# Gated recurrence, first head group: one filling piece behind each pair of heads instead of two behind all four

## What is computed

```python
def step(state, inp):                      # one chunk of 64 tokens
    qc, kc, vc, gc = inp
    b = jnp.cumsum(gc, axis=2)
    diff = b[:, :, :, None, :] - b[:, :, None, :, :]
    decay = jnp.exp(jnp.minimum(diff, 0.0)) * tri[:, :, None]
    A = jnp.einsum('bhtsd,bhsd->bhts', qc[:, :, :, None, :] * decay, kc)
    o = (jnp.einsum('bhts,bhsv->bhtv', A, vc)
         + jnp.einsum('bhtd,bhdv->bhtv', qc * jnp.exp(b), state))
...
o = o * lax.rsqrt(jnp.mean(o * o, axis=-1, keepdims=True) + RMS_EPS)
```

## Time and profile before

| what | value |
|---|---|
| median of 3 runs | 2115.13 us (2115.03 to 2115.35) |
| profiled execution, its own time | 2115.07 us |
| its span in the profile | 2113.3 us |
| granted TensorE clock, mean | 0.999 of full speed |
| PE (matmul) busy | 2089.2 us, 99% of the span |
| DVE busy | 894.8 us, 42% |
| ACT busy | 789.8 us, 37% |
| POOL busy | 868.0 us, 41% |

### The profile page before, as it was taken

How to read it: one execution, slowest core, us unless ns; L and a number is a source line. 1 busy time by engine, 2 the same in 40 slices (tenths; PEclk the granted TensorE clock), 3 DMA queues, 4 the chain that set the end, 5 groups by cost and what they waited for, 6 DMA issues and landing times.

```text
span 2113.3 us, 33496 instructions
## 1 busy us (share of the span) xinstructions
PE 2089.2 (99%) x13820; PEld 1741.6 (82%) x13820; DVE 894.8 (42%) x1653; ACT 789.8 (37%) x1611; POOL 868.0 (41%) x680
## 2 busy tenths in 40 slices
PE   8999999999999999999999999999999999999998
PEld 7878888778978888778888888888888888888886
DVE  6173565535373465526432211433422612222264
ACT  5424335554423325455422222345433432222244
POOL 4633433232543433233354444343444345454423
PEclk9999999999999999999999999999999999999999
DMA  7522223122222223122242332242233133332222
GB/s 247 178 65 80 78 67 100 41 80 80 80 82 80 77 68 100 41 81 70 76 144 83 118 98 83 89 135 80 66 114 100 61 110 101 109 108 92 100 70 90
DMA packets 98679, 196.65 MB, mean 93 GB/s; under 512 B 3680, under 2 KB 12256, under 8 KB 98144
## 3 DMA queue, kind: packets, MB, share of 16 engines
q1 hardware_dynamic: 95072, 183.25, 26.6%
q10 hardware_dynamic: 3456, 11.27, 1.5%
HBM read 192.41 MB, written 2.10 MB: 92 GB/s over the span
## 4 chain that ended last, share of the span: by engine, by line
PE 59%; ACT 1%; DVE 0%; issue 0%; DVEq 0%
PE ps L902 18%; PE ps L903 18%; PE ps L904 18%; PE ps L1017 1%; PE ps L1157 1%; PE ps L1025 0%; PE ps L1034 0%; PE ps L1180 0%; PE ps L1200 0%; PE ps L1189 0%; PE ps L1070 0%; PE ps L1052 0%; ACT L1581 0%; PE ps L974 0%; PE ps L1210 0%; PE ps L1062 0%
## 5 line engine op out<-in xcount | busy, mean ns | idle before, releaser
L851 POOL TENSOR_TENSOR wl<-raw,wh 128x512 fp32r<-128x512 f32 (+2 forms) x676 | 867.8, 1307 | 1220.6 <-ACT wh L1255 1210.8
L1255 ACT CAST wh<-raw 128x512 fp32r<-128x512 f32 (+2 forms) x692 | 380.7, 604 | 773.3 <-PE ps L904 672.8
L902 PE MATMUL ps<-xh,wh 128*128 128x512 f32 (+1 forms) x1376 | 514.2, 374 | 1.2 <-issue 1.2
L904 PE MATMUL ps<-xh,wl 128*128 128x512 f32 (+1 forms) x1376 | 509.1, 370 | 0.0
L903 PE MATMUL ps<-xl,wh 128*128 128x512 f32 (+1 forms) x1376 | 508.7, 370 | 0.0
L902 PEld LDWEIGHTS ps<-xh,wh 128*128 128x128 f32 x1376 | 259.4, 189 | 46.1 <-issue 3.9
L904 PEld LDWEIGHTS ps<-xh,wl 128*128 128x128 f32 x1376 | 259.1, 188 | 44.6
L903 PEld LDWEIGHTS ps<-xl,wh 128*128 128x128 f32 x1376 | 259.4, 188 | 42.1
L902 PE MATMUL ps<-wh,xh 128*128 128x512 f32 (+1 forms) x608 | 239.1, 393 | 0.2 <-issue 0.2
L904 PE MATMUL ps<-wh,xl 128*128 128x512 f32 (+1 forms) x608 | 234.4, 386 | 0.0
L903 PE MATMUL ps<-wl,xh 128*128 128x512 f32 (+1 forms) x608 | 234.4, 385 | 0.0
(11 more groups left out here) (273 smaller groups left out, 2436.2 us busy)
## 6 DMA issues: line engine op xcount, KB each, us to landing
raw<-w_in SPq DMA_DIRECT2D x58, 1024.0 KB, 5.2
raw<-w_out SPq DMA_DIRECT2D x20, 1024.0 KB, 5.0
raw<-f1g SPq DMA_DIRECT2D x10, 1024.0 KB, 5.1
raw<-f1u SPq DMA_DIRECT2D x10, 1024.0 KB, 5.1
raw<-f1d SPq DMA_DIRECT2D x10, 1024.0 KB, 5.0
raw<-f2g SPq DMA_DIRECT2D x10, 1024.0 KB, 5.2
raw<-f2u SPq DMA_DIRECT2D x10, 1024.0 KB, 5.1
raw<-f2d SPq DMA_DIRECT2D x10, 1024.0 KB, 5.1
```

What stands on the lines that cost most here:

```text
L851: pool.tensor_tensor(wl[s], raw[:, u % 2, k, 0:b.width], wh[s].bitcast(F32), ALU.subtract).then_inc(low_done, 1)
L902: pe.matmul(o, still[0], move[0], start=k0 + k == 0, stop=False)
L904: mm = pe.matmul(o, still[1], move[0], start=False, stop=k0 + k == b.ktiles - 1)
L1255: act.copy(wh[:, v % 3, k, 0:width], raw[:, v % 2, k, 0:width]).then_inc(high_done, 1)
```

## The change

The levels of the first head group are no longer together; the second group's stay so. It holds for levels 0 to 7 on PE, and for DVE's reading in levels 1 to 8, in both layers.

```diff
@@ -512,7 +512,7 @@
                            (states, 1), (read, 1), (gated, 4))
                 for ph in levels:
 
-                    ph.together = True
+                    ph.together = g == 1
                 for ph in levels + [turn, states, read, gated]:
                     add(ph)
                 add(Late(ahead))
```

## The result

Measured: 2126.61 us (median of 5 runs, 2123.43 to 2129.66) against 2115.03 us for the kernel before (5 runs, 2114.41 to 2115.35) on the same chip. The ratio is 1.0049, with a 95% interval from 1.0038 to 1.0061: slower by half a per cent. The forecast was 2123.0 us, the range 2117.0 to 2126.0. The sign and the mechanism came as forecast; the median lies 0.6 us above the upper end of the range, the ratio (which is taken against the runs of before beside it) inside it.

A forecast was written before the change was run, and what follows sets the result against it. PE's stream of matmuls was taken as the bound (busy 2089.2 of 2113.3 us). Switches +4.5, old waits -2.6 and new waits +6.0 gave +7.9 us, so 2123.0 us, range 2117.0 to 2126.0.

The forecast's parts named there:

- The switches: PE, first head group: 16 more groups of small products between large matmuls, 0.28 us each, +4.5 us.
- the half level: PE's time for two heads' small products, 12 large matmuls and the change back: 0.66 + 2.63 + 0.31 = 3.60 us.
- The estimate that the prediction worked out from the 25 ns: PE's added small-product groups would cost 3.5 us in place of 4.5; the prediction kept 4.5.
- The old waits: PE's waits for DVE at level 3's small products, one in each layer, would go: -2.6 us.
- The first burst: POOL's subtractions hold DVE's L1941 at level 2's second pair; PE starts 0.77 us late in each layer (bounds 0 and 1.5).
- The second burst: Level 4's first pair: copy and POOL's subtractions follow the same piece, DVE is held, PE waits 2.25 us in each layer.
- the second wait's bounds: PE's wait at level 4's first pair: 1.2 us if L1943 slips in early, 3.2 if one more instruction is held.
- Rival 3: New waits feed themselves: each of four half levels loses some 0.4 us more, 8 x 0.4 = 3.2; 2126 us, chance 0.10.
- PE waits elsewhere in the group: Sign against the prediction: PE waits in the first head group at places other than those forecast.
- under 2 us in all: Sign against the prediction: PE's waits for DVE's L1943 in the whole program stay under 2 us.
- a half level under 3.5 us: Sign against the prediction: PE's two-head share of a level, without wait, takes under 3.5 us.
- PE's busy time: Sign expected in the profile: PE is busy for about 4.5 us more in the whole program.

## Why the prediction was right, and where it fell short

**The switches.** Forecast 0.28 us a group, 4.5 in all. Measured 0.33 on the average (16 groups, 5.2 us) in the kernel with the copies where they were, 0.35 in the four outer levels, and 0.34 in the changed kernel itself (layer 2: 4.07 + 1.30 - 0.52 - 2.11 = 2.74 us for 8 groups, 5.5 in all). The term was 0.7 to 1.0 us small. The step behind it is the half level, taken as 3.60 us where it takes 3.62 to 3.64: a small error that stands twice in each level. The estimate that the prediction worked out from the 25 ns of the Trainium skill, "TensorE: Matmul & The Clock Gate", section "Wait — 56ns, not 53.3ns?", was 3.5 us and is farther off.

**The old waits.** They went, -2.6 us, in every kernel with PE's parted order; the trace of the one with the old DVE order shows none.

**The first burst.** Forecast 0.77 us at level 2's second pair; measured 0.52. L1941 at 123.05 was held for 0.57 us over its own 0.69, by the last subtraction alone, as forecast. The forecast held it for 0.76: counted from PE's products at 114.20, L1941 stood at 8.85 us and not at 8.73, and the burst was over at 9.56 and not at 9.63. PE also wanted the pair 0.1 us later, three half levels of 3.64 and not 3.60. Thinning POOL took the wait away.

**The second burst.** Forecast 2.25 us at level 4's first pair, measured 2.11. L1941, L1942 and L1943 took 1.52, 1.77 and 1.33 us where I had put 1.49, 1.7 and 1.38. Shown by three kernels: with POOL thin there the wait is 0, with all copies back it is 0, and with one copy moved it is 0 at this pair and 0.44 at the next. The rule of the Trainium skill, "SBUF — State Buffer", section "Who interferes with whom" (a Vector instruction with two SBUF inputs and a GpSimd one reading SBUF exclude each other for the whole instruction), was what chose 2.25 over 1.2. The trace agrees, with 1.33 us for an L1943 a quarter as large, and with 0.45 for the same instruction when POOL is thin.

**The sum.** 5.5 - 2.6 + 5.3 comes to 8.1 us before rounding, against 7.9 forecast; layer 2 of the first profile shows half of it undisturbed, 4.07. Two of the terms were off, in opposite ways, the switches by 0.7 to 1.0 us and the waits by 0.7 (6.0 against 5.3). That the sum came this close is in part luck.

**Where it fell short** is a sentence that isn't there. I costed the 2.25 us as a wait and nothing more. The step from the wait to the sum took for granted that TensorE's clock stays at 2.4 GHz, because it did so behind the 1.3 us waits of before. Behind the wait of 2.1 us it fell in 6 of the 8 layers profiled with that wait (once in the first profile, twice in each of two others, once in the thinned kernel), and each fall cost 1.4 to 1.6 us by the stretches. In the first profile, whose run is 0.2 us above the median, that is 1.43 us; 6 falls in 8 would be some 2 us of a run on the average. The upper end of my range, worked out from the second wait's bounds alone, has no room for it. Rival 3 had the size, 2126, but the wrong mechanism: the half levels behind a wait of 0.52 us took 3.64 and 3.63 us, so the waits did not feed themselves.

**The other part of the median** isn't the change's: the first product came 1.69 us late in the profiled run, behind the late load. The runs of the kernel before beside the experiments spread by as much (2114.85 to 2118.42 us in 60 runs), while the five beside the result all lie at 2115.35 or below. So the first ratio counts, in part, a late start as the change's. By the stretches the change costs 8.1 us, and 9.6 to 11.1 with the falls of the clock that the first two profiles show. I had said that a measurement can tell 0.2%; of that 4.2 us, 2.5 can be the heap that a few runs fall in.

**My check for being wrong** had "PE waits elsewhere in the group", "under 2 us in all" and "a half level under 3.5 us"; none happened. Of what the profile would show, PE's busy time is off: up by 6.7 us and not 4.5. By the terms above, some 5.5 of it are the switches, and the rest is about what the stretch at half clock took.

## What to carry to other kernels

When an engine reads out a result in order, behind other work, the place of the reading can decide more than its length: here 0.6 us of copy on the wrong side of an update was worth 1.7 us. Ask of every wait that is moved what else starts on the same event; the copy and POOL's burst both hung on the end of one piece, and each alone was harmless. On a kernel whose TensorE is 99% busy, allow 3.5 us for a new wait of 2, since a fall of the clock behind it cost some 1.5 us more in 6 of 8 cases here, and read the layer's own stretch in the trace rather than the time of the run.

## What was not expected of the hardware

TensorE's clock went to 1.2 GHz behind waits of 2.1 us in 6 of 8 cases, at 1.4 to 1.6 us each, behind the early wait of 1.93 to 2.48 us in 4 of 6, and behind the stops of 1.8 and 1.9 us in both. In the levels of the kernels that have no longer wait there than 1.3 us it never did: two waits in each profile of the kernel before and of the one with the outer levels parted (1.3 us), two in the one with later copies (0.7), four in the one with a copy moved (up to 0.53). The same instruction stream with the same wait to 0.01 us could have a fall or not; what decides is open. The other surprise is PE's stop of 1.8 to 1.9 us amid small products with no wait that the profile names, in both layers of one kernel only.
